# A decoder trunk with product-key retrieval: top-k of each pass's first tile by heads, the next trunk beside the other tiles' top-k, and TensorE's row sums between trunk jobs

## The reference, cut to what matters

```python
q = einsum('td,de->te', t, w_pq)                  # 8 heads x 2 halves x 128
s = einsum('thpk,hpnk->thpn', q, sub_keys)        # 128 scores per head and half
s1, i1 = top_k(s[:, :, 0], 16); s2, i2 = top_k(s[:, :, 1], 16)
cand = s1[..., :, None] + s2[..., None, :]        # 256 per head
top_s, pos = top_k(cand, 16)                      # 16 experts of 16384 per head
g = softmax(top_s)
a = gelu(einsum('td,ted->te', tb, peer_u[idx]))   # 128 dots per token
out = einsum('te,ted->td', g * a, peer_v[idx])    # 128 rows summed per token
```

## Time and profile before

| | |
|---|---|
| median of 3 runs (lowest, highest) | 4753.07 us (4751.09, 4753.92) |
| the profiled execution, its span | 4759.94 us, 4758.2 us |
| PE busy | 3426.1 us, 72% |
| DVE busy | 3227.6 us, 68% |
| POOL busy | 2819.9 us, 59% |
| ACT busy | 856.6 us, 18% |
| moved by DMA | 1527.14 MB, 1208.11 of it gathers; mean 321 GB/s |
| granted TensorE clock, mean | 0.84 |

### The profile page before, as it was taken

The page is one execution under the profiler, slowest core; times in us unless marked ns, Lnnn a source line. Parts: engine busy times, 40 slices in busy tenths (PEclk is TensorE's granted clock), DMA queues, the critical chain, the costliest instruction groups (busy, mean ns, idle before and its releaser), DMA issues.

```text
span 4758.2 us, 38594 instructions
## 1 busy us (share of the span) xinstructions
PE 3426.1 (72%) x12244; PEld 2329.1 (49%) x12244; DVE 3227.6 (68%) x5950; ACT 856.6 (18%) x2508; POOL 2819.9 (59%) x2317
## 2 busy tenths in 40 slices
PE   8998558898887665766677457989898466555554
PEld 7887416566875223655466225656785122111111
DVE  2101488867757888787668888776756987666665
ACT  1001121121201221112121121122212222111111
POOL 0000066666547677676557776665656677777775
PEclk9999788999678898888788788999769798666766
DMA  6444388999989898999999987999989889999997
GB/s 197 142 138 130 110 318 291 384 358 387 348 299 380 318 326 290 379 395 388 366 365 387 381 300 272 374 357 361 383 297 328 295 326 331 371 367 372 362 371 297
DMA packets 604898, 1527.14 MB, mean 321 GB/s; under 512 B 43412, under 2 KB 293460, under 8 KB 604696
## 3 DMA queue, kind: packets, MB, share of 16 engines
q0 software_dynamic: 331776, 1208.11, 68.0%
q1 hardware_dynamic: 272920, 316.58, 19.6%
HBM read 1517.29 MB, written 7.23 MB: 320 GB/s over the span
## 4 chain that ended last, share of the span: by engine, by line
PE 40%; POOL 21%; DMA 15%; DVE 13%; issue 9%; ACT 1%; SPq 1%; DVEq 0%; another core or an unknown queue 0%; ACTq 0%; POOLq 0%
PE ps L678 22%; POOL urow L625 11%; POOL vrow L625 11%; PE ps L691 10%; DMA vrow<-in_peer_v_dram,idx 6%; DMA W<-in_w_in_dram 4%; DMA W<-in_w_b_out_dram 3%; DVE urow L1112 3%; PE ps L830 2%; DVE X L1123 2%; PE ps L870 2%; DMA urow<-in_peer_u_dram,idx 1%; PE ps L791 1%; PE ps L667 1%; DVE RB L1214 1%
## 5 line engine op out<-in xcount | busy, mean ns | idle before, releaser
L625 POOL DMA_INDIRECT urow<-in_peer_u_dram,idx x1152 | 1451.1, 1260 | 1495.9 <-DVE idx L1221 612.8
L1112 DVE CUSTOM_DVE_ANT_0 urow<-urow,T 128x1024 f32<-128x1024 f32 x1152 | 1402.6, 1221 | 544.2 <-DMA urow<-in_peer_u_dram,idx 387.9
L625 POOL DMA_INDIRECT vrow<-in_peer_v_dram,idx x1152 | 1366.8, 1186 | 415.0 <-issue 340.6
L870 PE MATMUL ps<-vrow,RV 128*128 128x512 f32 x1584 | 964.0, 743 | 804.2 <-DMA vrow<-in_peer_v_dram,idx 745.0
L678 PE MATMUL ps<-RH,W 128*128 128x256 f32 (+1 forms) x4608 | 1184.0, 418 | 206.4 <-DMA W<-in_w_in_dram 63.6
L678 PEld LDWEIGHTS ps<-RH,W 128*128 128x128 f32 x4608 | 900.7, 197 | 469.2 <-issue 84.6
L1123 DVE SCALAR_TENSOR_TENSOR X<-vrow,wts,X 128x1024 f32<-128x1024 f32 x756 | 971.9, 1286 | 154.7 <-issue 111.9
L870 PEld LDWEIGHTS ps<-vrow,RV 128*128 128x128 f32 x1584 | 323.1, 225 | 1442.0 <-issue 1225.5
L901 ACT ACTIVATE gel<-dots 128x4 f32<-128x4 f32 x288 | 58.2, 202 | 1518.6 <-DVE dots L1112 1222.6
L691 PE MATMUL ps<-W,RB 128*128 128x256 f32 (+1 forms) x1152 | 263.5, 390 | 33.2 <-issue 27.6
L678 PE MATMUL ps<-RB,W 128*128 128x256 f32 (+1 forms) x1024 | 265.3, 413 | 28.7 <-DMA W<-in_w_b_out_dram 26.4
(11 more groups left out here) (174 smaller groups left out, 2273.5 us busy)
## 6 DMA issues: line engine op xcount, KB each, us to landing
W<-in_w_in_dram SPq DMA_DIRECT2D x112, 1024.0 KB
W<-in_w_pq_dram SPq DMA_DIRECT2D x32, 1024.0 KB
urow<-in_peer_u_dram,idx POOLq DMA_INDIRECT x1152
vrow<-in_peer_v_dram,idx POOLq DMA_INDIRECT x1152
W<-in_w_a_out_dram SPq DMA_DIRECT2D x16, 1024.0 KB
W<-in_w_b_out_dram SPq DMA_DIRECT2D x16, 1024.0 KB
W<-in_w_mix_o_dram SPq DMA_DIRECT2D x16, 1024.0 KB
W<-in_w_xq_dram SPq DMA_DIRECT2D x16, 1024.0 KB
```

Of the source, the lines that this page charges most:

```text
L625: return pool.indirect_dma_start(ring[:, slot, :], None, table, bass.IndirectOffsetOnAxis(ap=idx[:, q % TSLOT, e:e + 1], axis=0))
L870: o = pe.matmul(ps[:, bank + b, :], diag[:, pe_turn[m] % NDIAG, :], vrow[:, m % NV, b * 512:(b + 1) * 512], start=m in pe_first, stop=m in ...
L1112: dve.tensor_tensor_reduce(urow[:, m % NU, :], urow[:, m % NU, :], T[:, q % TSLOT, :], 1.0, 0.0, ALU.mult, ALU.add, dots[:, n % WRING, m % ...
```

## The change

1. **Top-k by heads for the first tile of each pass.** `top_head(p, h)` does head h's whole selection as soon as its scores are in SBUF, up to `idx` and, one head later (`weigh_head`), the gate weights. `emptied((p, "sc", h))` stands in front. ACT gets one exponential per head (`head_exp`). POOL waits for indices per head (16 picks), not per tile. Pass 0's picks begin with its first head: its scores are placed at the steps 0, 0, 5, 10, 15, 21, 27, 33, the next trunk starts at step 38 (FIRST). In the later passes the last 56 steps (CLOSE) before a pass's start hold query columns, scores and heads, the last scores 9 steps before it.
2. **The other tiles' top-k as asides.** `top_k` is now a generator; VectorE's `peer_to` calls `aside_to(step)`, which does the pieces that are due: over 64 steps (WIDE) from step 38 or 3 of passes 0 and 2, over 40 steps a tile from step 0 and 40 of passes 1 and 3. The next trunk runs in the same steps: from 38 in pass 0, from 3 in passes 1 and 2 (in pass 1 only up to the `v` jobs by step 80, the `c` jobs start at 82).
3. **TensorE sums between jobs.** `peer_products` goes. After each trunk job TensorE does the sums of all steps before the place of the job just done. Spans lie in banks 6 and 7 (4 and 5 too in pass 3); jobs planned beside them get six banks. 418 picks are summed on TensorE (66, 128, 28, 196 by pass, 56, 92, 56, 192 before). Six diagonals, in a tensor of their own, made three steps early.
4. **Room.** `S` is three separate places (RB, KV, RB), `sgT` and `ln_b` move. `sg_b` is no longer spread over the partitions: it is loaded as 8 rows (`SGB`), and TensorE adds it with a matmul against a row of the identity in the `mx` job. The query columns of head 1 (`pq` 2 and 3), which stood before head 0's scores, now stand behind them with those of head 2 (`queries_before`).

```diff
-NDIAG = 4
+NDIAG = 6
-HEAD = 36
-CLOSE = 36
-OVER = 4
+FIRST = 38
+HEAD = 40
+WIDE = 64
+CLOSE = 56
+OVER = 3
+DIAG_EARLY = 3
...
+def topk_window(p, i):
+    if p % 2:
+        return step_base(p) + HEAD * (i - 1), step_base(p) + HEAD * i
+    first = step_base(p) + (FIRST if p == 0 else OVER)
+    return first, first + WIDE
...
     for p in range(2 * DEPTH):
         b, n = pick_base(p), pass_picks(p)
-        head = HEAD * (len(GROUPS[p % 2]) - 1) - LAG
+        head = max(head_steps(p) - LAG, 0)
         if p + 1 < 2 * DEPTH:
-            span(b, b + head, step_base(p) + head + LAG)
-            span(b + n + LAG - CLOSE, b + n, step_base(p + 1) + LAG)
+            if head:
+                span(b, b + head, step_base(p) + head + LAG + 1)
+            span(b + n - CLOSE, b + n, step_base(p + 1) + 2, lambda m: p % 2 or m % 2)
             continue
...
-                        if picks[m][1] == 0:
-                            pool.wait_ge(idx_done, picks[m][0] + 1)
+                        if m == 0 or turn_of_pick(m) > turn_of_pick(m - 1):
+                            pool.wait_ge(idx_done, turn_of_pick(m))
...
             def end(ins):
                 ins.then_inc(job_done, 1)
+                if len(started) < len(jobs):
+                    peer_to(STARTS[jobs[len(started)][0]])
+
+            def peer_to(n):
+                while summed[0] < len(on_pe_picks):
+                    m = on_pe_picks[summed[0]]
+                    if sum_step(m) >= n:
+                        return
...
+                    pe.wait_ge(diag_done, pe_turn[m] + 1)
+                    pe.wait_ge(v_in[m % NV], 16 * (m // NV + 1))
+                    for b in range(2):
+                        o = pe.matmul(ps[:, bank + b, :], diag[:, pe_turn[m] % NDIAG, :],
+                                      vrow[:, m % NV, b * 512:(b + 1) * 512],
+                                      start=m in pe_first, stop=m in pe_last)
+                    o.then_inc(v_on_pe, 1)
+                    summed[0] += 1
...
+            def top_head(p, h):
...
+                emptied((p, "sc", h))
+                Sh = S[0][:, h * 256:(h + 1) * 256]
...
+                both(lambda j: dve.max(m[j][:, 0:8], part[j]))
+                both(lambda j: dve.max_index(i[j][:, 0:8], m[j][:, 0:8], part[j]))
+                breathe()
...
+                ch.link(dve.max(best[:, 0:8], Sh))
+                ch.link(dve.max_index(place[:, 0:8], best[:, 0:8], Sh))
+                ch.link(dve.match_replace(Sh, best[:, 0:8], Sh, LOWEST))
...
                 norm(2)
-
-            def all_top_k(p):
-                emptied(LAST_SC[p])
-                for i in range(len(GROUPS[p % 2])):
-                    top_k(p, i)
+                for h in range(PH):
+                    top_head(p, h)
+                weigh_head(p, PH - 1)
```

More of the change, by code:

```diff
@@ L153, in plan_jobs @@
         mine = phase_jobs(p % 2)
-        total, past = sum(j[3] for j in mine), 0.0
-        start = step_base(p - 1) + HEAD * (len(GROUPS[(p - 1) % 2]) - 1) if p else 0
-        end = step_base(p) - CLOSE if p else 0
+        place = places(p)
         names = [j[0] for j in mine]
@@ L165, in plan_jobs @@
                 held = ("kb", 0, 0) in names[:k + 1] and ("ss",) not in names[:k]
-                top = 6 if held else 8
+                since = max(place[k - 1] if k else 0, step_base(p - 1) + 1 if p else 0)
+                summing = any(a <= place[k] + 2 and since <= b + 1 for a, b in held_by_sums) or name[1] in ("pq", "sc")
+                top = 6 if held or summing else 8
                 cursor += cursor % width
@@ L177, in plan_jobs @@
             turn[name] = counts[owner]
-            past += cost
-            ahead[name] = start + round((end - start) * past / total) if p else 0
-    return jobs, index, bank, before, turn, ahead
+            ahead[name] = place[k]
+            starts[name] = max(place[k - 1] if k else 0, step_base(p - 1) + 1 if p else 0)
+    return jobs, index, bank, before, turn, ahead, starts
 def plan_units(index):
@@ L264, in decoder_step @@
         of[m] = len(of)
-    span_end = {after - 1: i for i, (first, after, bank, step) in enumerate(spans)}
     pe_first = {min(m for m in on_pe if on_pe[m] == i): i for i in range(len(spans))}
@@ L1044, in trunk @@
                 for h in range(PH):
[L1045 removed]
+                    for c in queries_before(h):
                         evac((p, "pq", c), qp[c // 2 % 2][:, c % 2, 0:n], pf((p, "pq", c)))
@@ L1095, in merge @@
                 dve.wait_ge(v_on_pe, max(pe_turn[m] for m in on_pe if on_pe[m] == k) + 1)
-                before = [dve_turn[m] for m in dve_turn if m < after]
+                before = [dve_turn[m] for m in dve_turn if sum_step(m) < step]
                 if before:
@@ L1141, in peer_to, with aside_to @@
                             merge(k)
+                    aside_to(steps[0])
+            asides, going = [(p, i) for p in range(2 * DEPTH) for i in range(1, len(GROUPS[p % 2]))], []
+            def aside_to(n):
+                while asides:
+                    p, i = asides[0]
+                    if not going:
+                        going.append([0, top_k(p, i)])
+                    k, work = going[0]
+                    if topk_steps(p, i, k) > n:
+                        return
+                    going[0][0] += 1
+                    if next(work, "end") == "end":
+                        going.pop()
+                        asides.pop(0)
             def emptied(name):
```

320 lines of the change are left out of this document (208 added, 112 removed).

## The result

The changed kernel takes 4635.31 us (median of 4 runs, 4626.19 to 4640.8), against 4753.49 for the kernel before measured beside it (4 runs, 4751.09 to 4756.76): a ratio of 0.9748, 95% interval 0.9733 to 0.9763, so 2.5% faster. The profiled execution took 4635.82 (span 4633.8), 124 us less than that of before, where I had forecast 145 less.

What follows compares the result with a forecast made beforehand. No engine bounds the whole; each stage has its own limit (VectorE, TensorE, DMA or POOL's gathers). Terms -97 + 20 + 19 - 24 - 52 - 11 = -145 took 4759.9 to 4615, less 6.9 to 4608, stated as 4605; range 4500 to 4710.

Steps and rivals of the forecast that it cites:

- Start, -97: Pass 0, start to step 38: first dot at 502 us, step 38 at 624 instead of 721, 97 us less.
- The bias "within 5 us": Trunk's mx stage: bias moves from VectorE to an 8-row matmul, a 0.5 MB broadcast load goes; effect within 5 us.
- 38 to 102, +20: Pass 0, steps 38 to 102: tile 1's top-k beside the trunk, VectorE 251 us at 88%, 285 us, 20 longer.
- 102 to 208, 0: Pass 0, steps 102 to 208: same jobs over the same steps, bound by TensorE, no change.
- Score stages, +19, -27, +23: Last stretches of passes 0, 1 and 2, scores and heads together: 19 us longer, 27 shorter, 23 longer.
- VectorE at 92%: Last stretches of passes 0 and 2: VectorE's work at 92% busy sets the time, 199 and 193 us.
- Rival C, the hand-over: Score stages: heads wait for sums, query columns, scores and copies; 8.8 us open per head, 4826 us, slower; chance 0.13.
- Pass 1, -24: All of pass 1: stages of 254, 689 and 174 us, together 1117 against 1140.9, 24 less.
- the added wait: Pass 1's v jobs: long TensorE jobs keep the v-row ring full, so POOL waits a few us for each.
- Pass 2, -52: All of pass 2: trunk starts at step 3, not 36; stages change by -75 and +23, 52 us less.
- Pass 3, -11: Pass 3's first 80 steps of top-k and sums: VectorE 200 us at 84%, 239 against 250, 11 less.
- The heads, 79 us a tile: First tiles' top-k by heads: 9.86 us of VectorE per head, 79 per tile against 53.6 for a whole tile.

Runs made afterwards that it cites:

- e1_no_bias: Changed kernel without the spatial gate's bias sg_b and its 8-row matmuls: 4626.95 us, 0.9715 of the kernel before.
- e2_bias_128: Changed kernel with the bias operand padded with zeros to 128 rows, all its matmuls kept: 4629.98 us, 0.9716 of the kernel before.
- e11_even_heads: Changed kernel with the heads of passes 1 to 3 spaced evenly over the last stretch before each pass: 4633.84 us, 0.9746 of the kernel before.
- e6_all_pe: Changed kernel with all row sums of the last stretches of passes 0 and 2 on TensorE: 4638.36 us, 0.9765 of the kernel before.
- e3_sums_inside: Changed kernel with TensorE also doing due row sums between the quarters of a v job: 4633.27 us, 0.9715 of the kernel before.
- e10_os_cost: Changed kernel with the planned cost of the eight sample attention output jobs at 6.5, not 2: 4634.16 us, 0.9765 of the kernel before.
- e12_together: Changed kernel with the edits of e2_bias_128, e3_sums_inside, e10_os_cost and e11_even_heads together: 4598.29 us, 0.9689 of the kernel before.
- e8_tilewise_all: Changed kernel with whole-tile top-k for all first tiles, pass 0's picks after all its scores: 4712.5 us, 0.9937 of the kernel before.
- e7_tilewise: Changed kernel with whole-tile top-k for the first tiles of passes 1 to 3 only: 4644.19 us, 0.9788 of the kernel before.

## Why the prediction was right, and where it was not

The forecast was 4605 for 4635.31 measured. Its mechanism held where the gain lies, in the start, and in the direction of each later stage; what it names as the bound of the score stages and of pass 2 is not borne out. It is 30 us off: 21 in the sum of its terms, 6 because this profiled execution stands 0.5 us above its median where that of before stood 6.9 above, and 3 that I had rounded off. That the sum came so near is in part luck: term by term the misses come to some 90 us in one direction (the start, pass 1's first part, pass 2's first 210 steps, pass 3's first steps) and 70 in the other, 25 of these in the two stretches forecast at nothing.

**Start, -97: mis-sized by 20.** The first dot is at 516.0, not 502, and step 38 comes 128.4 us later, not 122. The bias "within 5 us" was priced as VectorE's gain against one matmul of a known kind, and I priced the matmul at nothing without a row for its shape; in the first trunk no engine's work is beside it, and its stage took 21.0 us and not 8.1. e1_no_bias and e2_bias_128 give it 16 us by the ratios. The first query columns ran at a clock of 0.76, and TensorE was busy with them for 9.35 us instead of 7.04:

```profile
488.00:498.00 10.00, 9.35 (x32) 7.50 (x32) 0.24 (x1) 0.70 (x2) 0.00 (x0) 0.76 0.37 115
```

Head 0's 9.3 us were near the forecast. The first dot came 6.2 us after its gather left, not 4.4, behind a wait of 5.3 us for head 1's scores and head 1's first searches. The steps then took 6 us more than forecast: seven heads (64 us) and 38 dots (47) keep VectorE at 108.8 of 128.4 us, 85% rather than 95%, with 13.5 us of waits for u rows.

**38 to 102, +20: right** (+14.3), and VectorE came out as forecast: 245.4 (forecast 251) of 277.6, at 88%. But TensorE is at 95%, so that VectorE bounds the stage isn't shown.

**102 to 208, 0: wrong by 15, open in part.** The same steps took 15 us less, and in every run below 7 to 26 (429 to 447 against 454.6). The bound that I named, TensorE, moved with it. Before:

```profile
984.50:1439.10 454.60, 402.03 (x1757) 331.58 (x1757) 305.61 (x392) 93.45 (x238) 273.17 (x211) 0.81 0.95 351
```

TensorE was busy for 402.0 us before and 383.4 after. It isn't quite the same work: the next pass's query columns began 10 us ahead of step 208 before (1429.2) and right at it after (1361.05), which is 8 us of it. The rest went with a clock of 0.83 and not 0.81; e11_even_heads and e6_all_pe, whose TensorE was busy for 398 us at 0.80, took 447. Why the clock differed stays open, and no run was made for it.

**Score stages, +19, -27, +23: right** (+13.7, -32.4, +10.2), 5, 5 and 13 better than forecast. VectorE was at 85, 76 and 87%, not at 92: a head cost it 74.3/8 = 9.3 us, not 9.86, and in e6_all_pe, with 33 us less of VectorE's time in the end of pass 0, that stage is 6 us shorter (TensorE is then full at 98%). So "VectorE at 92%" gave about the right size, and no run shows that VectorE bounds them. What does stays open in passes 0 and 2: query columns, copies, heads and the gathers may all have a part in it; e6_all_pe and e11_even_heads moved it by 7 us at most. In pass 1's last stretch it was TensorE that was nearly full, 158.4 us of 169.0.

**Rival C, the hand-over.** It needed 6 us of open time per head. In the last stretch of pass 1 of the changed kernel VectorE waited for score copies 12.0 us in all, 1.5 per head, in the ends of passes 0 and 2 3.9 and 8.5:

```profile
DVE urow L1223 <- DMA urow<-in_peer_u_dram,idx: 22.7, 18, 2.7
DVE m L1384 <- ACT KV L1163: 12.0, 6, 3.7
```

**Pass 1, -24: the total was off by 11, its parts by more.** The first part missed by 31 us: the added wait, told as a few us and costed at nothing, is 16 to 20 (e3_sums_inside). The remaining 15 are VectorE's share, 82% with the ring free (220.2 of 269.3) instead of 88%. The c jobs' stage ran at 385 GB/s, not 379, and was 16 better than forecast.

**Pass 2, -52: measured -35.5.** Steps 0 to 67 took 262.8 us, not 290: VectorE was at 96%, and its 251 us were 10 less than forecast. Steps 67 to 210 took 546.8, not 493. TensorE was busy for 452, 18 more than my 69% share of its work, and idle for 95, where 88% leaves 59. The share assumed a cost spread evenly over the steps; the real jobs aren't, but the plan's costs set right (e10_os_cost) gave 537.5 us, and 543.1 in e12_together, against 544 to 556 in the ten kernels with the same plan: so uneven jobs are at most a small part of the 54, and the cause of the rest stays open. The clock was 0.78 there (0.85 in the earlier trace rows), which goes with the longer busy time.

**Pass 3, -11: nothing** (-1.3): VectorE at 81% of the stage, not 84%.

**The heads, 79 us a tile:** measured 74.3, against 53.1 for a whole tile in e8_tilewise_all. By the rule of the Trainium skill ("VectorE: DVE Perf Modes", section "The TRN2 errata") I had estimated 71; the measured (74.3 - 53.1)/110 = 0.19 us per added instruction lies between that and my rows. That the rule speaks against the change mattered less than either price: e7_tilewise, without the added time in passes 1 to 3, is no faster.

**A reading put right.** 379 GB/s isn't one of the two highest rates of the earlier trace rows: the last 80 us of pass 0's trunk had 391, beside the 394 of pass 1. The argument for pass 1 doesn't rest on it.

## What to carry to other kernels

Work that is moved into a stage costs only what the stage's other floors leave uncovered: find the floor with the moved work taken out (here the gathers' 1.43 us each), not only the busy sum of the engine that does it. When an in-order engine also gives back a ring's buffers between its own long jobs, compare the job's length with what the ring covers, and put the releases inside the job if it is longer. When TensorE is alone on the path, a few-row operand that alternates with 128-row ones is worth padding with zeros to their row count.

## What the runs showed of the hardware that was not expected

- Matmuls of 8 rows alternating with matmuls of 128 rows (both 128 columns, float32) started 0.42 us apart at full clock; the same ones with 128 rows each 0.22 us apart. With the alternation the granted clock fell to 0.50 in 165 to 182 us though TensorE was busy for 11.93 of the last 12.5 us; without it, it stayed at 1.00 over the whole stage.
- 128-row gathers left POOL one after another with 0.30 us between them, 1.38 to 1.43 us from one to the next with VectorE half idle (71 in 97.7 and in 101.6 us), the same as in the long pure stretch of pass 3 (477 in 681.6 us).
- In the kernel before, too, two 128-row matmuls (128 columns, float32, full clock) took 0.65 us from start to start between 64-row ones, and 0.47 among their like.
- The last stretch of pass 3, the same in all kernels, differed by 17 us (709 to 726) between executions: more than most effects looked for here, so the single stages decided, not the totals.
